# Latent attention turned round: keys on partitions, row maxima from a rounded pass, exact scores in three rounded products

## The reference, cut to what matters

```python
def mla_attend(q_nope, q_rope, k_nope, k_rope, v):
    s = (jnp.einsum('bqhd,bkhd->bhqk', q_nope, k_nope, preferred_element_type=jnp.float32)
         + jnp.einsum('bqhr,bkr->bhqk', q_rope, k_rope, preferred_element_type=jnp.float32)) * MLA_SCALE
    p = jax.nn.softmax(s, axis=-1).astype(v.dtype)
    return jnp.einsum('bhqk,bkhd->bqhd', p, v)
# in even_mixer
y_mla = o_ml * jax.nn.silu(mg_l)
```

## Time and profile before

| | us |
|---|---|
| median of 3 runs | 2779.68 |
| the runs | 2771.91, 2779.93, 2779.68 |
| the profiled execution | 2777.8 |
| its span | 2776.0 |
| TensorE busy in the span | 2422.2 (87%) |
| VectorE, ScalarE, GpSimd busy | 1575.8, 1156.4, 209.7 |

### The profile page before, as it was taken

The page is one execution under the profiler, slowest core; times in us unless marked ns, Lnnn a source line. Parts: engine busy times, 40 slices in busy tenths (PEclk is TensorE's granted clock), DMA queues, the critical chain, the costliest instruction groups (busy, mean ns, idle before and its releaser), DMA issues.

```text
span 2776.0 us, 29543 instructions
## 1 busy us (share of the span) xinstructions
PE 2422.2 (87%) x12162; PEld 1860.4 (67%) x12162; DVE 1575.8 (57%) x2049; ACT 1156.4 (42%) x1591; POOL 209.7 (8%) x188
## 2 busy tenths in 40 slices
PE   4978799796999999992399996889999979399998
PEld 4856565572888888882287775736777768288887
DVE  4488267435899999994510117555444455623275
ACT  3154256401788888881411233233333331412231
POOL 2000012001011111110000000010000005000004
PEclk9999999998999999996699995799999979699999
DMA  3101010329899999995100000001000020311131
GB/s 107 47 29 46 0 62 1 129 69 409 320 382 381 383 385 393 396 380 217 61 16 27 31 16 1 20 25 52 1 1 1 1 84 1 116 46 46 46 152 53
DMA packets 98867, 342.23 MB, mean 123 GB/s; under 512 B 21260, under 2 KB 46645, under 8 KB 71080
## 3 DMA queue, kind: packets, MB, share of 16 engines
q1 hardware_dynamic: 84776, 310.37, 29.5%
q0 software_dynamic: 10448, 17.28, 1.7%
q10 hardware_dynamic: 3504, 12.63, 1.2%
HBM read 323.41 MB, written 33.60 MB: 129 GB/s over the span
## 4 chain that ended last, share of the span: by engine, by line
PE 77%; DVE 12%; ACT 6%; DMA 3%; issue 1%; POOL 0%; SPq 0%; PEldq 0%; DVEq 0%; ACTq 0%; POOLq 0%
PE psm L230 71%; PE psm L2752 3%; DVE mem L911 1%; PE psm L1670 1%; DMA mem<-y2d 1%; ACT r L461 1%; DMA mem<-in_ada_w_dram 1%; DVE mem L2527 1%; PE psm L1031 1%; ACT mem L1101 1%; DVE r L337 1%; DVE small L371 1%; DVE small L370 1%; DVE mem L1145 1%; PE psm L1693 1%
## 5 line engine op out<-in xcount | busy, mean ns | idle before, releaser
L230 PE MATMUL psm<-r,r 128*128 128x512 f32 (+3 forms) x6766 | 1575.1, 394 | 94.8 <-DVE r L337 47.1
L230 PEld LDWEIGHTS psm<-r,r 128*128 128x128 f32 (+2 forms) x6766 | 1256.2, 187 | 388.3 <-DVE r L337 33.6
L230 PE MATMUL psm<-mem 128*128 128x64 f32 (+15 forms) x3574 | 608.1, 388 | 44.1 <-ACT mem L2312 12.0
L337 DVE TENSOR_TENSOR r<-mem,r 128x1024 fp32r<-128x1024 f32 x448 | 524.8, 1220 | 178.5 <-ACT r L328 173.4
L230 PEld LDWEIGHTS psm<-mem 128*128 128x128 f32 (+6 forms) x3574 | 391.4, 195 | 155.7 <-issue 80.1
L328 ACT ACTIVATE r<-mem 128x1024 fp32r<-128x1024 f32 x448 | 441.1, 1053 | 18.7 <-DMA mem<-in_w_in_dram 10.1
L2811 DVE COPY mem<-psm 128x512 f32<-128x512 f32 (+1 forms) x128 | 71.4, 558 | 175.8 <-PE psm L2752 175.8
L445 PE MATMUL psm<-cst,mem 128*128 128x128 f32 x208 | 40.2, 361 | 117.6 <-ACT mem L431 93.0
L2752 PEld LDWEIGHTS psm<-cst,mem 128*128 128x128 f32 x640 | 70.9, 147 | 100.9 <-DVE mem L2811 56.7
L2771 ACT ACTIVATE mem<-psm 128x512 f32<-128x512 f32 x64 | 38.2, 597 | 220.4 <-PE psm L2752 220.4
L2752 PE MATMUL psm<-cst,mem 128*128 128x128 f32 x640 | 109.5, 286 | 11.2 <-DVE mem L2811 7.7
(11 more groups left out here) (332 smaller groups left out, 1758.4 us busy)
## 6 DMA issues: line engine op xcount, KB each, us to landing
mem<-in_exp_w_gate_dram SPq DMA_DIRECT2D x64, 1024.0 KB, 7.3
mem<-in_exp_w_up_dram SPq DMA_DIRECT2D x64, 1024.0 KB, 7.6
mem<-in_exp_w_down_dram SPq DMA_DIRECT2D x64, 1024.0 KB, 7.2
mem<-in_ada_w_dram SPq DMA_DIRECT2D x16, 1024.0 KB, 14.4
mem<-in_odd_w_in_dram SPq DMA_DIRECT2D x10, 1024.0 KB, 6.4
mem<-in_even_w_in_dram SPq DMA_DIRECT2D x9, 1024.0 KB, 5.4
mem<-in_x_dram SPq DMA_DIRECT2D x16, 512.0 KB, 8.1
mem<-in_w_in_dram SPq DMA_DIRECT2D x8, 1024.0 KB, 5.2
```

What stands on the lines that cost most here:

```text
L230: return p.e.matmul(o, l, r, start=start, stop=stop, skip_group_check=True)
L337: p.e.tensor_tensor(l, mem(kb + 8, [R * n])[:, w * q:w * q + w], h.bitcast(F32), SUB).then_inc(*self.lo_done.up(i, q))
```

## The change

What it does:
- The loop now runs over 80 steps: head pair (4), query half (2), key tile of 128 (10). Keys lie on partitions, 512 queries on the free axis, so the weights need no transpose. Two heads are done in a step.
- Queries and keys are split into a rounded part (ScalarE, QHI/KHI) and the rest (VectorE, QLO/KLO, written over QT/KT). Scores are the sum of three rounded products, hi x hi, hi x lo, lo x hi.
- The softmax needs a row maximum per query. A product of the rounded parts alone, queries on partitions, gives 1280 scores per row; VectorE reduces them. Sixteen such products (8 query tiles, 2 heads) make a pair's. Their negatives are transposed by TensorE, copied, and a DMA per head lays them as one row of 1024; it becomes row 96 of the rounded queries, against a row of ones in the rounded keys, so that the first of the three products subtracts it.
- Exp (512 wide, scale only) goes to PT, four buffers. The denominators: GpSimd adds five key tiles of weights up in SUMS, TensorE multiplies SUMS by ones twice per half, ScalarE takes Ln and Exp(-x), VectorE multiplies the result by it and by MG.
- Values: per head of the pair a float32 matmul with 64 columns of weights, into partitions 0 to 63 or 64 to 127 of one bank.
- The maxima of pair p + 1 are computed during the loop of pair p (`prepare_*` run step by step, one or two steps at a time by `beside`); those of pair 0 during the up-projection, which is reordered (`UP`) so that pair 0's heads come first, and confined to five banks.
- `mg` is computed with channels on partitions; the count of matmuls and Silu is the same.
- SP's loads of X from x2d wait for the last scores instead of the end of the up-projection.
- An unrelated tile UP is renamed UPC.

The core of the diff (renamings and memory places left out; lines of "..." mark cuts):

```diff
@@ up_sync
-            p.wait_ge(*up_pe.at("mv", 9))
-            p.wait_ge(*up_dve.at("qr", 3))
+            for hp in range(4):
+                for hd in range(2):
+                    p.wait_ge(*ml_act.at("tops", hp))
+                    p.e.dma_start(mem(48 + 4 * (2 * hp + hd), [1024], p=97)[96:97, :], TOPT[8 * hd:8 * hd + 8, :]).then_inc(*top_in[hd].up(hp))
+            p.wait_ge(*ml_pe.at("s", 79, 1))
@@ order of the up-projection; each engine's loop follows it
+        UP = [("kn", 0, 0), ("qn", 0, 0), ("rope", 0, 0), ("rope", 0, 1), ("kn", 1, 0), ("qn", 1, 0), ("kn", 2, 0), ("qn", 2, 0),
+              ("kn", 3, 0), ("qn", 3, 0), ("rope", 1, 0), ("rope", 1, 1)] + [("mv", i, 0) for i in range(10)]
+        FIRST = (("kn", 0), ("qn", 0), ("rope", 0))
...
+                if (name, a) not in FIRST:
+                    run(first, 2)
+            run(first, 100)
@@ the maxima, one generator per engine
+        def prepare_scalar(p, hp):
+            for hd in range(2):
...
+                p.e.activation(KHI[hp % 2][hd][0:96, :], KT[:, h, :], ACT.Copy).then_inc(*ml_act.up("k", h))
+                p.e.activation(QHI[hp % 2][hd][0:96, :], QT[:, h, :], ACT.Copy).then_inc(*ml_act.up("q", h))
+                yield
+            for _ in range(18):
+                yield
+            p.wait_ge(*ml_pe.at("tops", hp))
...
+            p.e.activation(TOPT, PB.ps("tops", hp)[0:16, 0:128], ACT.Copy).then_inc(*ml_act.up("tops", hp))
...
+            p.wait_ge(*top_in[1].at(hp))
+            p.e.activation(QHI[hp % 2][1][96:97, :], ..., ACT.Copy).then_inc(*ml_act.up("row", hp))
+        def prepare_vector(p, hp):
+            yield
+            p.wait_ge(*up_pool.at(7))
+            for hd in range(2):
...
+                p.e.tensor_tensor(KLO[h][0:96, :], KT[:, h, :], KHI[hp % 2][hd][0:96, :].bitcast(F32), SUB).then_inc(*ml_dve.up("k", h))
...
+                p.e.tensor_tensor(QLO[h][0:96, :], QT[:, h, :], QHI[hp % 2][hd][0:96, :].bitcast(F32), SUB).then_inc(*ml_dve.up("q", h))
+                if hp < 2:
+                    p.e.tensor_copy(KHI[hp][hd][96:97, :], cst("ones")[96:97, 0:1].broadcast_to([1, 1280])).then_inc(*ml_dve.up("ones", hp, hd))
+                yield
...
+            for n in range(16):
+                p.wait_ge(*ml_pe.at("m", hp, n))
+                p.e.tensor_reduce(TOP[:, n:n + 1], PSM[:, 5:8, :].rearrange("p a b -> p (a b)")[:, 0:1280], AX, MAX).then_inc(*ml_dve.up("m", hp, n))
...
+                yield
...
+        def prepare_tensor(p, hp):
+            for _ in range(3):
+                yield
+            for n in range(16):
...
+                for q, (o, w) in enumerate(((0, 512), (512, 512), (1024, 256))):
+                    ps = take_bank(p, MBK[q], "m", hp, n, q)
+                    last = mm(p, ps[:, 0:w], QHI[hp % 2][hd][0:96, 128 * qt:128 * qt + 128], KHI[hp % 2][hd][0:96, o:o + w], True, True)
+                last.then_inc(*ml_pe.up("m", hp, n))
+                yield
...
+        def beside(i):
+            return 2 if i in (3, 5, 7, 9, 11) else 1
@@ the loop
+        def scores_of_pair(p, t):
...
+                ps = take_bank(p, SBK[hd], "s", t, hd)
...
+                mm(p, ps[:, :], KHI[P][hd][0:97, k0], QHI[P][hd][0:97, s0], True, False)
+                mm(p, ps[:, :], KHI[P][hd][0:96, k0], QLO[h][0:96, s0], False, False)
+                mm(p, ps[:, :], KLO[h][0:96, k0], QHI[P][hd][0:96, s0], False, True).then_inc(*ml_pe.up("s", t, hd))
+        def latent_tensor(p):
...
+            for t in range(len(STEPS) + 6):
+                if t < 80:
...
+                    scores_of_pair(p, t)
+                    run(ahead)
+                if 0 <= t - 2 < 80:
+                    values_tensor(p, t - 2)
+                if t < 80:
+                    run(ahead, beside(t % 20) - 1)
+                if 0 <= t - 5 < 80 and STEPS[t - 5][2] in (4, 9):
+                    sums_tensor(p, t - 5)
+        def values_tensor(p, t):
...
+                last = mm(p, ps[64 * hd:64 * hd + 64, :], MV[:, i, v0:v0 + 64], PT[t % 4][:, hd, :], i == 0, i == 9)
+        def sums_tensor(p, t):
...
+            p.wait_ge(*ml_pool.at(t))
+            for hd in range(2):
+                last = mm(p, ps[64 * hd:64 * hd + 64, :], cst("ones")[:, 0:64], SUMS[:, hd, :], i == 4, i == 9)
+            last.then_inc(*ml_pe.up("sum", t))
+        def latent_scalar(p):
...
+                    for hd in range(2):
+                        p.wait_ge(*ml_pe.at("s", t, hd))
+                        if t >= 4:
+                            p.wait_ge(*ml_pe.at("pv", t - 4))
+                            p.wait_ge(*ml_pool.at(t - 4 if STEPS[t - 4][2] % 5 else t - 3))
+                        p.e.activation(PT[t % 4][:, hd, :], PB.ps("s", t, hd), ACT.Exp, scale=SCALE).then_inc(*ml_act.up("e", t, hd))
+                        PB.frees(("s", t, hd), ml_act.at("e", t, hd))
+                    run(ahead, beside(t % 20))
...
+        def latent_pool(p):
+            for t, (hp, half, i) in enumerate(STEPS):
+                if i % 5:
...
+                    if i % 5 == 1:
+                        if t > 5:
+                            p.wait_ge(*ml_pe.at("sum", t - 2))
+                        a = PT[(t - 1) % 4]
+                    else:
+                        p.wait_ge(*ml_pool.at(t - 1))
+                        a = SUMS
+                    p.e.tensor_tensor(SUMS, a, PT[t % 4], ADD).then_inc(*ml_pool.up(t))
```

More of the change, by code:

```diff
@@ L2586, in up_sync @@
                 p.e.dma_start(X[:, i, :], x2d[i]).then_inc(*x_in[i].up("x2"))
+        FIRST = (("kn", 0), ("qn", 0), ("rope", 0))
+        UB = (0, 1, 2, 3, 4)
         def up_tensor(p):
+            first = prepare_tensor(p, 0)
             gla_done(p)
             for half in range(2):
-                ps = take(p, "kr", half)
+                ps = take(p, "kr", half, order=UB)
                 lk_there(p)
@@ L2647, in up_vector @@
+            run(first, 100)
         def up_vector(p):
+            first = prepare_vector(p, 0)
             gla_done(p)
@@ L2696, in build @@
         YM = mem(147, [4, 1024])
-        PP = [mem(163, [1280]), mem(168, [1280])]
-        PT = [mem(192, [10, 128]), mem(142, [10, 128])]
-        OT = [mem(173, [512]), mem(197, [512])]
-        NM, RS2, RI = small(8), [small(8), small(8)], small(8)
         SCALE = 96.0 ** -0.5
-        its = [(qt, h) for qt in range(8) for h in range(8)]
-        ml_pe, ml_act, ml_dve = sig("mla_pe"), sig("mla_act"), sig("mla_dve")
+        QHI = [[rounded(kb, 1024) for kb in m] for m in ((0, 4), (13, 17))]
+        KHI = [[rounded(kb, 1280) for kb in m] for m in ((8, 27), (21, 163))]
+        QLO, KLO = [rounded(48 + 4 * h, 1024) for h in range(8)], [rounded(80 + 5 * h, 1280) for h in range(8)]
+        PT = [mem(kb, [2, 512]) for kb in (168, 172, 192, 196)]
+        SUMS = mem(142, [2, 512])
+        RSUM = mem(120, [512])
+        TOP = small(16)
+        TOPT = mem(146, [128], p=16)
+        STEPS = [(hp, half, i) for hp in range(4) for half in range(2) for i in range(10)]
+        ml_pe, ml_act, ml_dve, ml_pool = sig("mla_pe"), sig("mla_act"), sig("mla_dve"), sig("mla_pool")
+        top_in = [load("top0_in"), load("top1_in")]
+        SBK, MBK = (0, 1), (5, 6, 7)
         def up_done(p):
@@ L2745, in latent_tensor @@
[L2745 to L2760 removed]
+            ahead = iter(())
@@ L2781, in latent_scalar @@
-            turn_out_scalar(p, late)
-        def soften_scalar(p, s):
-            qt, h = its[s]
-            p.wait_ge(*ml_dve.at("max", s))
-            if s >= 2:
-                p.wait_ge(*ml_pe.at("pt", s - 2, 2))
-            if qt >= 2:
-                p.wait_ge(*ml_dve.at("ri", qt - 2))
-            p.e.activation(PP[s % 2], scored(s), ACT.Exp, bias=NM[:, h:h + 1], scale=SCALE, accum_out=RS2[qt % 2][:, h:h + 1]
-                           ).then_inc(*ml_act.up("e", s))
-            for q in range(3):
-                PB.frees(("s", s, q), ml_act.at("e", s))
@@ L2819, in row_max_vector @@
[L2819 to L2839 removed]
+            p.wait_ge(*ev_act.at("mg", 3, 768))
@@ new lines, in latent_vector @@
+            ahead = iter(())
+            for t in range(len(STEPS) + 6):
+                if t < 80:
+                    if t % 20 == 0:
+                        run(ahead, 100)
+                        ahead = prepare_vector(p, t // 20 + 1) if t < 60 else iter(())
+                    run(ahead, beside(t % 20))
+                if 0 <= t - 5 < 80 and STEPS[t - 5][2] == 9:
+                    hp, half, i = STEPS[t - 5]
+                    y = YM[:, hp, 512 * half:512 * half + 512]
+                    p.wait_ge(*ml_pe.at("pv", t - 5))
+                    p.wait_ge(*ml_act.at("r", hp, half))
+                    p.then(p.e.tensor_tensor(y, PB.ps("pv", hp, half), RSUM, MUL), ml_dve, "o", hp, half)
+                    PB.frees(("pv", hp, half), ml_dve.at("o", hp, half))
+                    p.e.tensor_tensor(y, y, MG[:, hp, 512 * half:512 * half + 512], MUL).then_inc(*ml_dve.up("y", hp, half))
```

370 lines of the change are left out of this document (189 added, 181 removed).

## The result

| | before | after |
|---|---|---|
| median (4 runs each, same chip) | 2778.20 | 2810.99 |
| range | 2771.91 to 2779.93 | 2810.34 to 2818.47 |
| span of the profiled execution | 2776.0 | 2809.4 |

The ratio is 1.0128, 95% interval 1.0104 to 1.0152: slower by 1.3%. The forecast of no change was wrong. The time is near that of the rival "the clock is lost longer", 2815.

A forecast was written before the change was run, and what follows sets the result against it. The chain was 77% TensorE's, with hardly any slack in the loop. Loop -58.4, up-projection +36 and clock +19.6 gave -3 us; from the profiled execution, adjusted to the median, 2777 us, forecast's own range 2755 to 2795.

The forecast's parts named there:

- forecast of no change: Whole kernel: 2777 us, no difference over 0.3% (8.3 us) showing; own range 2755 to 2795, chance 0.45.
- the clock is lost longer: Rival, loop waits and chain of maxima: 3.4 us of clock per wait, 10 more in up-projection, 2815; chance 0.24.
- the chain of maxima: Up-projection: 15 reductions for pair 0, each product waiting for the one before, 49.4 us in all.
- The wait behind GpSimd: Loop, after steps 9, 14, ...: TensorE stands 3.65 us until GpSimd's addition and ScalarE's exp end; 14 times, 51.1 us.
- The tail: Loop's end, behind the last exp: four GpSimd additions in a row, sums, Ln, Exp, two VectorE operations; 15.5 us.
- half clock for 2.8 us costs 1.4: Loop, behind each of 14 waits: half clock costs 19.6 us in all, with ends 0 and 48.
- the middle one: Of three earlier gaps (3.58, 2.41, 2.67 us), the 2.41 one, granted clock 0.63 for 3.6 us, taken for the clock's price.
- A step's TensorE work: Loop, each of 80 steps: scores 1.37, value pair 0.89, shape change 0.17; 2.43 us, 194.4 in all.
- Value pairs: Loop: two 64-column fp32 matmuls into bank halves run together, 0.89 us per pair; otherwise 1.75.
- Maxima and start of a pair: Loop, pairs 1 to 3: products 31.0 us, waits 14.7, pair starts beside GpSimd 9 (between 0 and 27).
- Up-projection: Stage ahead of the loop: pair 0's maxima move in, scores begin near 1907; 36 us more, between 20 and 55.
- The loads of X delaying nothing: SP's x2d loads, issued 16 us before the loop's end: X has landed by the output weights' landing, nothing late.

The follow-up runs named there:

- the version without the wait: Changed kernel with TensorE's read of SUMS for step t at the end of step t + 2 instead of t + 5: 2732.54 us, ratio 0.9836.
- the best version: Changed kernel with SUMS read at t + 2, paired values, two bank sets, one maximum per item, rows of ones by ScalarE: 2697.18 us, ratio 0.9709.

## Why the prediction was wrong

Every mechanism that it names was found: the wait, the half clock behind it, the chain of maxima, the halves that run together. What failed are sizes, three of them too small: TensorE's work in a step (14.2 us over the loop), the clock (11.2) and the up-projection (8.4). The first two, with 6.0 from maxima and starts and a few smaller differences, turn a gain of 39 us in the loop into one of 12. Step by step, against its own numbers:

- **The wait behind GpSimd: right.** Its place, its chain and its number (14) are as written; its length is 3.26, not 3.65, because the addition takes 2.34 there (2.41 on average) where the row gave 2.72: 45.6 instead of 51.1. The tail is 18.5 where the terms give 17.0.
- **Clock: the mechanism right, the size off.** The step "half clock for 2.8 us costs 1.4" failed. It cost 30.8, 2.2 per wait and 2.6 where nothing hid it, instead of 19.6. The gap of 3.58 in the earlier trace rows, nearest in length, would have given 3.4 per wait, 48 in all and 17 too much; the middle one that I took was 11 too little. No row gave this price, only its ends of 0 and 48 held.
- **A step's TensorE work: 2.61, not 2.43; the largest miss.** The change of shape was read from one direction in one place, 0.17, and taken for both; there and back it is 0.35. Rounded matmuls came at 0.234 instead of 0.228, the value pair at 0.86 instead of 0.89. Over 79 steps 14.2 us.
- **Value pairs: right.** The halves run together; one after the other they would be 1.72.
- **Maxima and start of a pair:** with the Ln and Exp 56.8 predicted; the version without the wait leaves 290.9 - 79 x 2.61 - 12.9 (15 sums) - 9.0 (tail) = 62.8. Of the 6.0 more, 4.0 are the starts of pairs, whose gaps there are 7.19, 2.88 and 2.88 us, 13.0 instead of 9. I had counted two subtractions beside GpSimd and forgotten the casts, which stretch too. By the Trainium skill (SBUF — State Buffer, Who interferes with whom), cited in the prediction, the upper end, 27, was to be nearer. The measured 13.0 is over the 9 taken, so the direction is right, but the end of 27 is far off.

  The loop's account: 348.9 predicted with the clock; + 14.2 (step) + 6.0 (maxima, starts) - 0.4 (sums) - 5.5 (wait) + 11.2 (clock) + 1.5 (tail) = 375.9.
- **Up-projection: +44.4, not +36.** The last reduction starts 56.1 us after the first (49.4 predicted), at half clock for much of it (0.77 from 1850 to 1917). First scores at 1917.45, not 1907.
- **The loads of X delaying nothing: right for this kernel**, because its tail is long. It stopped being right when the tail became short.
- **The sum.** The gain was overstated by 27 and the cost by the up-projection understated by 8: 35 us, which is the distance from 2777 to the measured time. The rival that ended slower had named the bound, 2.2 us of clock per wait, and that is what they came out at. That its time, 2815, was nearly met is in part luck: it had 3.4 per wait, 10 us more in the up-projection, and a step of 2.43; the shorter loss of clock was made up by the longer step.

So the new arrangement can shorten the loop by 114 us (387.7 to 273.4 in the best version), and the changed kernel loses most of that in one place, the step in which SUMS is read. Moving that alone is worth 78 us.

## What to carry to other kernels

Where a helper engine adds up in one buffer, ask in which step the reader of that buffer stands, and who waits for the next addition: read five steps late, it stalled ScalarE, then TensorE, and the stall took two thirds of its own length in clock on top. Price a wait of TensorE with its clock, as a range: here the gaps of the kernel before gave 0 to 3.4 us, waits of 2.41 us cost anything from nothing to 3.1, and waits of 0.7 nothing. When a stage gets shorter, look at the transfers behind it again, since they may have been hidden only by what was removed.

## What was not expected of the hardware

- Two waits of 2.41 us in like surroundings, one followed by 1.5 us of loss to the clock and one by none; a third lost 3.1. Two of three waits of 1.64 us were followed by half clock as well, none of the nine of 0.7 was.
- A one-row cast of 1280 elements on VectorE took 2.85 to 2.89 us beside GpSimd's additions and 0.82 otherwise: an operation on one partition stretches as those on 96 do (in the earlier trace rows it was 0.69 to 1.81).
- GpSimd's addition of 128x1024 took 2.34 to 2.37 us in the changed kernel's loop when VectorE did nothing beside it (28 of 64), whether SUMS was an input or not, and up to 3.38 otherwise; in the output projection of the kernel before, with VectorE active beside each, it was 2.72. That VectorE makes the difference is not shown by a run of its own.
- Two float32 matmuls of 64 columns into the two halves of a bank take 0.86 us, two of 128 columns 1.72.
